# Evacuating the last RWKV columns as they come, and making the wide products after them

## The reference

```
rwkv_cols = (h @ w_in)[...]                               # 26 column tiles of 128
mixed = rwkv_cols + (prev - rwkv_cols) * mu               # token shift
r, kc, vc, wd, ad, gd = split(mixed)
decay, a_lr, g_rw = ...(wd, ad, gd)                       # three small products (LoRA)
kk = kc * k_k;  kc = kc * (1 + (a_lr - 1) * k_a)
kk = kk / max(norm(kk), 1e-12)                            # per head of 64
yr, state = rwkv7_scan(r, decay, kc, vc, kk, kk * a_lr, state)
bonus = sum(r * kc * r_k, per head) * vc
out_c = (head_norm(yr) * lnx_g + lnx_b + bonus) * g_rw
```

## Time and profile before

| | |
|---|---|
| median of 3 runs | 3082.54 us |
| the runs | 3073.86, 3082.54, 3086.95 us |
| the profiled execution | 3080.22 us, its span in the trace 3078.4 us |
| mean granted clock of TensorE | 0.956 of full speed |
| PE busy | 2850.6 us, 93% of the span |
| DVE busy | 1744.5 us, 57% |
| ACT busy | 1252.9 us, 41% |
| POOL busy | 521.0 us, 17% |

### The profile page before, as it was taken

The page is one execution under the profiler, slowest core; times in us unless marked ns, Lnnn a source line. Parts: engine busy times, 40 slices in busy tenths (PEclk is TensorE's granted clock), DMA queues, the critical chain, the costliest instruction groups (busy, mean ns, idle before and its releaser), DMA issues. The chain is left out here.

```text
span 3078.4 us, 63316 instructions
## 1 busy us (share of the span) xinstructions
PE 2850.6 (93%) x25694; PEld 2654.5 (86%) x25694; DVE 1744.5 (57%) x2611; ACT 1252.9 (41%) x1753; POOL 521.0 (17%) x340
## 2 busy tenths in 40 slices
PE   8998989989889999899999988989899899998998
PEld 7997888777688998799999978987777889987998
DVE  4444754586676665544354458445855866655444
ACT  4534522244332443444354355222533334434543
POOL 0003650054310000000000046400543100000000
PEclk9999999999998999899999999999999989999999
DMA  4444340144374556344444443401353744663443
GB/s 173 150 147 141 123 137 18 29 125 175 98 302 144 179 211 225 128 149 149 138 142 150 144 136 114 127 24 31 116 182 99 294 161 167 216 217 135 149 150 127
DMA packets 120689, 448.08 MB, mean 146 GB/s; under 512 B 13761, under 2 KB 24161, under 8 KB 112929
## 3 DMA queue, kind: packets, MB, share of 16 engines
q1 hardware_dynamic: 99072, 331.09, 32.4%
q0 software_dynamic: 21408, 114.03, 10.1%
HBM read 397.04 MB, written 48.02 MB: 145 GB/s over the span
## 5 line engine op out<-in xcount | busy, mean ns | idle before, releaser
L1548 ACT ACTIVATE w_high<-ring 128x1024 fp32r<-128x1024 f32 x597 | 630.8, 1057 | 737.3 <-PE gemm_banks L916 308.2
L912 PE MATMUL gemm_banks<-in_high,w_high 128*128 128x320 f32 (+1 forms) x2720 | 802.4, 311 | 23.8 <-ACT w_high L1548 11.9
L1973 DVE TENSOR_TENSOR w_low<-ring,w_high 128x1024 fp32r<-128x1024 f32 x436 | 532.7, 1222 | 468.8 <-ACT w_high L1548 468.4
L913 PE MATMUL gemm_banks<-in_low,w_high 128*128 128x320 f32 (+1 forms) x2720 | 794.8, 308 | 0.0
L748 POOL TENSOR_TENSOR w_low<-ring,w_high 128x1024 fp32r<-128x1024 f32 x162 | 414.8, 2563 | 1204.4 <-ACT w_high L1548 1203.3
L912 PEld LDWEIGHTS gemm_banks<-in_high,w_high 128*128 128x128 f32 x2720 | 514.6, 189 | 30.1 <-DVEq L2280 12.9
L913 PEld LDWEIGHTS gemm_banks<-in_low,w_high 128*128 128x128 f32 x2720 | 514.3, 189 | 1.7
L916 PE MATMUL gemm_banks<-in_high,w_low 128*128 128x320 f32 (+1 forms) x2720 | 449.2, 307 | 6.3 <-POOL w_low L748 3.9
L916 PEld LDWEIGHTS gemm_banks<-in_high,w_low 128*128 128x128 f32 x2720 | 407.4, 188 | 8.3 <-POOL w_low L748 4.9
L959 PE MATMUL gemm_banks<-in_high,w_high 128*128 128x320 f32 x640 | 208.8, 339 | 22.5 <-DVE arena L2099 16.7
L986 PE MATMUL gemm_banks<-act_high,w_high 128*128 128x320 f32 x704 | 208.5, 311 | 2.5 <-DVE arena L2022 2.5
(11 more groups left out here) (420 smaller groups left out, 4238.4 us busy)
## 6 DMA issues: line engine op xcount, KB each, us to landing
ring<-in_w SPq DMA_DIRECT2D x598, 512.0 KB, 3.5
arena<-in_kc POOLq DMA_DIRECT2D x14, 1024.0 KB, 6.7
arena<-in_vc POOLq DMA_DIRECT2D x14, 1024.0 KB, 7.7
out_fill<-stage SPq DMA_DIRECT2D x80, 160.0 KB, 3.8
arena<-in_ssm POOLq DMA_DIRECT2D x16, 512.0 KB, 13.2
out_s_ssm<-arena POOLq DMA_DIRECT2D x16, 512.0 KB, 14.1
arena<-in_ret POOLq DMA_DIRECT2D x16, 512.0 KB, 22.4
out_s_ret<-arena POOLq DMA_DIRECT2D x16, 512.0 KB, 6.0
```

The source lines that it names most:

```text
L912: mm(dst, w_high[:, slot, w(k)], in_high[:, k, 0:n], start=(k == 0), stop=False)
L913: mm(dst, w_high[:, slot, w(k)], in_low[:, k, 0:n], start=False, stop=False)
L1548: f(w_high[:, slot], ring[:, s, 0:D], ACT.Copy).then_inc(weights_high, 1)
L1973: tt(w_low[:, slot], ring[:, pos % RING, 0:D], w_high[:, slot].bitcast(F32), ALU.subtract).then_inc(weights_split, 1)
```

## The change

The three steps that stood at columns 22, 23 and 24 are rearranged. The eight small products E3 are spread over columns 22 to 25 (two, one, one, four), and all wide products of columns 23 to 25, which now stand in a function of their own, are made after column 25 is evacuated. PE no longer waits for `mixed` before the head sums, and POOL waits for `rk` in the place of `mixed` before it issues the store of the shift state. No instruction is added or removed on any engine's computing part; the wait of PE is the only one that goes.

```diff
+BONUS_AT = {22: (0, 1), 23: (2,), 24: (3,), 25: (4, 5, 6, 7)}
...
                 fill("fill_rwkv", 0, AHEAD + 2)
-                pool.wait_ge(pre_v.sem, pre_v.value["mixed"])
+                pool.wait_ge(pre_v.sem, pre_v.value["rk"])
                 pool.dma_start(outs["shift"][l], sh_out).then_inc(dma["shift_stored"][0], 16)
...
                 need(pre_v, "rk")
-                need(pre_v, "mixed")
                 tile_sums(pre_p, "rks", K("bones"), E3)
...
-                if c == 22:
-                    for i in range(KT):
-                        ins_ = stt(E3[:, i], rr[:, i], PR("r_k", i), kk_[:, i], ALU.mult, ALU.mult)
-                        V_(ins_) if i < KT - 1 else V_.mark(ins_, pre_v, "rk")
-                if c == 23:
-                    ar0, kkc, ec = AR[:, :, 0:NCH, 0], chunks64(Bt[:, :, 0:TP]), chunks64(E[:, :, 0:TP])
-                    V_(tt(ar0[:, :, :, 1:C64], kkc[:, :, :, 1:C64], ec[:, :, :, 0:C64 - 1], ALU.mult))
-                    V_(copy(ar0[:, :, :, 0], kkc[:, :, :, 0]))
-                    V_(copy(pend, ec[:, :, :, C64 - 1]))
-                if c == 24:
...
-                    V_(tt(kk_, kk_, LW, ALU.mult))
+                for i in BONUS_AT.get(c, ()):
+                    ins_ = stt(E3[:, i], rr[:, i], PR("r_k", i), kk_[:, i], ALU.mult, ALU.mult)
+                    V_(ins_) if i < KT - 1 else V_.mark(ins_, pre_v, "rk")
                 if c == RT - 1:
-                    V_.mark(tt(Bt, Bt, Aa, ALU.mult), pre_v, "mixed")
...
+                    products_rwkv()
+
+            def products_rwkv():
+
+                (b0, b1), (r0_, r1_), (v0, v1) = sum_spans(), spans(rr), spans(vv)
+                ar0, kkc, ec = AR[:, :, 0:NCH, 0], chunks64(Bt[:, :, 0:TP]), chunks64(E[:, :, 0:TP])
+                V_(tt(ar0[:, :, :, 1:C64], kkc[:, :, :, 1:C64], ec[:, :, :, 0:C64 - 1], ALU.mult))
+                V_(copy(ar0[:, :, :, 0], kkc[:, :, :, 0]))
+                V_(copy(pend, ec[:, :, :, C64 - 1]))
+                ar0 = AR[:, :, NCH, 0].rearrange("p a (b t) -> p a b t", t=SL)
+                kkc, ec = (v[:, :, TP:T].rearrange("p a (b t) -> p a b t", t=SL) for v in (Bt, E))
+                V_(tt(ar0[:, :, :, 1:SL], kkc[:, :, :, 1:SL], ec[:, :, :, 0:SL - 1], ALU.mult))
+                V_(copy(ar0[:, :, :, 0], kkc[:, :, :, 0]))
+                V_(copy(pends, ec[:, :, :, SL - 1]))
+                V_(tt(kk_, kk_, LW, ALU.mult))
+                V_.mark(tt(Bt, Bt, Aa, ALU.mult), pre_v, "mixed")
+                need(pre_p, "rks")
+                V_(tt(r0_, b0, v0, ALU.mult))
+                V_.mark(tt(r1_, b1, v1, ALU.mult), pre_v, "bonus")
+                arrived(dve, layer, "x_stored")
+                arrived(dve, layer, "shift_stored")
```

More of the change, by code:

```diff
@@ L2125, in prepare_rwkv @@
             def prepare_rwkv(c):
-                (b0, b1), (r0_, r1_), (v0, v1) = sum_spans(), spans(rr), spans(vv)
                 if c in (16, 18):
@@ L2153, in prepare_rwkv @@
-                if c == 24:
[L2154 to L2158, removed]
-                    V_(tt(kk_, kk_, LW, ALU.mult))
-                if c == RT - 1:
-                    V_.mark(tt(Bt, Bt, Aa, ALU.mult), pre_v, "mixed")
[L2162 to L2166, removed]
+                for i in BONUS_AT.get(c, ()):
+                    ins_ = stt(E3[:, i], rr[:, i], PR("r_k", i), kk_[:, i], ALU.mult, ALU.mult)
+                    V_(ins_) if i < KT - 1 else V_.mark(ins_, pre_v, "rk")
```

## The result

The changed kernel took 3043.54 us (median of 4 runs, 3037.74 to 3057.67) against 3078.20 us for the kernel before (4 runs), a ratio of 0.9915 with a 95% interval of 0.9886 to 0.9944. It was measured twice more, beside the kernel before: 3046.53 against 3074.77 us (0.9901, 0.9878 to 0.9925) and 3055.52 against 3071.51 us (0.9945, 0.9926 to 0.9963; 12 runs). The differences of the medians are 34.7, 28.2 and 16.0 us; weighted by the runs of the changed kernel (4, 4, 12) they make 22.2 us. The prediction had 22.8. The prediction was stated as a time, from a kernel before at 3082.54 us: as ratios its 3060 is 0.993 and its range 0.990 to 0.997, and 0.9915 lies within, while the bare 3043.54 lies 7.5 us under the range.

What follows compares the result with a forecast made beforehand. PE was taken as the bound, through idle stretches and low clock before the head sums. Saving 11.38 us a layer, 22.8 in two, from the 3082.54 us median gave 3059.7, said as 3060; range 3051 to 3073.

Steps and rivals of the forecast that it cites:

- The sum on PE: PE, last column to head sums: both pauses and low-clock fills together save 11.38 us a layer, 22.8 us in two.
- The first pause: PE's idle time before fill 0: 0.74 us of 2.14 go, the other 1.4 stay.
- the second pause: PE's idle time before the third fill, 389.70 to 396.17: predicted to go whole, 6.47 us.
- The clock over the pause that is left: PE at fill 0 after 1.4 us idle: no loss of clock taken; bound on the other side 1.62 us.
- The weights of fills 1 to 3: ACT's high parts and POOL's splits for these fills come about when PE wants them: 0 us lost.
- The far bound of 5.1 us a layer: Worst case for the splits of fills 1 to 3: 4.93 us each, together 5.1 us lost a layer.
- `rk`: DVE's mark after the small products: set between 383.1 and 389.5, wanted by PE at 394.4, so no cost.
- The wide products: On DVE behind `rk`: 14.5 us, ending at 404.0, with DVE's idle time before the scan shrinking to 9.8.
- POOL's wait: POOL's 2.98 us wait for `mixed` goes; the split of fill 4 behind it is wanted only after the head sums.
- Hidden anyway: Rival 3: PE reaches the scan 11.4 us earlier but waits there; time stays at 3078 to 3087. Chance 0.11.
- DVE becomes the bound: Rival 4, before the scan: lateness beyond 9.8 us costs; gain gone at 21.2, 3098 us at 28.9. Chance 0.04.
- The clock ate nothing of the gain: Rival 2: splits or clock eat part before the head sums; far end 4.7 us gain a layer, 3073. Chance 0.16.

Runs made afterwards that it cites:

- the run with nine clearings: The changed kernel with the clearing of Ys on DVE before the scan made nine times in place of once: 0.9998 (0.9979 to 1.0016).

## Why the prediction came out as it did

**The sum on PE** was right. The first pause went to 1.34 us on the prediction's count (379.85 to 381.19, of which the timeline has 1.14 as idle), predicted 1.4; fills 0 to 3 ran at full clock, the second pause went whole, and the stretch is 15.95 and 16.00 us against about 15.5. That is 21.8 us in place of 22.8. The rest lies in the fills, which took 14.6 us a layer (381.19 to 395.80) and not 14.1: in fills 0 and 1 the low pass began 2.5 us after the fill's first matmul, where 2.35 is full pace, and in fill 1 it began at 387.47, just when its split was done (POOL starts the next one at 387.38).

**The clock over the pause that is left.** No loss was right: in 11 profiles with a pause of 0.9 to 1.4 us before fill 0, in both layers, fill 0 never slowed. Longer pauses differ: of ten of 1.9 to 2.0 us, before fill 0 or at column 23, seven brought the lower clock with its full loss (in one of them it began 1.4 us after the pause), three did not.

**The weights of fills 1 to 3.** The split of fill 1 came some 0.2 us late, no stall of a size that matters, as taken. The far bound of 5.1 us a layer was not needed.

**`rk`** was set at 387.76, that is 386.8 on the scale of the prediction, between its bounds of 383.1 and 389.5.

**The wide products** were mis-sized: 18.5 us and not 14.5. I took over their length from the kernel before, where some of them met no split. Behind column 25 POOL's splits follow each other closely, and four of the eight products are stretched: L2153 to 4.35 us (2.26 without a split), and the copies at L2154, L2155 and L2159 to between 2.3 and 2.9 (0.2 without). Two of these copies end at 394.49 and 400.36, each within 0.1 us of the end of a split (394.42 and 400.26). The Trainium skill (SBUF — State Buffer, SBUF: two separate sides) has the loser of the port wait for the whole instruction, and these rows agree. `rk` was early, so the bonus came only 1.4 us later than counted (405.4 on the prediction's scale), and the small products behind it took 0.8 us more than before, so that DVE's reserve is 8.03 us and not 9.8. It cost nothing here, and the run with nine clearings shows from where it would have.

**POOL's wait** I put down as one that "goes", with a split behind it that PE wants late. It is worth more: kept at `mixed`, it takes 8.3 us of the gain by the trace.

**What I had not separated.** The prediction treats the spreading and the moving as one cause. The runs show that each alone frees the third fill: DVE evacuated column 25 at 395.9, only 8.5 us after PE would have wanted that bank (387.4 in the prediction), and deferring either the small products or the wide ones makes that up. Moving most of the wide ones is needed for nothing that the trace shows, and it uses reserve (8.03 us are left, and 11.57 where they stay).

**The rivals.** "Hidden anyway" did not come: the scan starts earlier by what the head sums gain (DVE's first instruction of it at 440.22 less 0.95, against 450.20: 10.9 us). "DVE becomes the bound" did not come, and its point was misplaced by 1.8 us. The clock ate nothing of the gain, and the splits some 0.2 us a layer.

**Open.** The three sets give 34.7, 28.2 and 16.0 us by the medians around one stage gain of 21.8, and the intervals of the second and the third set (23.1 to 37.5 and 11.4 to 22.7 us) do not meet, so sets differ by more than one set's interval tells. The scan rows tie part of a single profile's surplus to the granted clock; why the clock of the scan differs from run to run was not found.

## What to carry to other kernels

Where one engine evacuates for another and also prepares later work, compare its backlog at each evacuation with the moment when the next tile wants that bank, and defer only as much as clears it; here either of two deferrals did. When work is deferred, look for waits that name its mark on every queue, because a wait that was free in the old order (0.9991 without it) can cost the whole gain in the new one (1.0002 with it). Price moved work by what will run beside it at its new place, not by what it took at the old.

## What the runs showed of the hardware

DVE and POOL take turns by the instruction: a DVE copy of 32 elements lasts 0.2 us in a gap of POOL's and 2.3 to 2.9 beside its splits, and the eight wide products last 11.7 us where POOL stands at a wait for most of them, and 18.5 where it works on. A pause of PE of 2.0 us took the granted clock to 0.54 in one layer and left it at 1.00 in the other layer of the same execution.
